# Hybrid decoder step with a mixture of 32 experts: the routing gap reordered, and expert weights fetched in pairs of chunks

## The reference, cut to what matters

```python
g_sel = argmax(hf @ w_rg + b_rg)                        # 1 of 4 groups
e_in  = (hf @ w_re + b_re).reshape(t, 4, 8)[tok, g_sel]
top_v, top_i = lax.top_k(e_in, 2)                       # 2 of its 8 experts
gate  = softmax(top_v) * g_prob[tok, g_sel]
expert = g_sel * 8 + top_i
# for each of 32 experts, on the tokens that chose it:
y = (silu(x @ w1[e]) * (x @ w3[e])) @ w2[e]             # w1, w3: 1024x512, w2: 512x1024
x = x + g2 * sum_k gate_k * y_k
out = rms_norm(x, final_norm_g)
```

## Time and profile before

| | |
|---|---|
| median of 3 runs | 1625.86 us (1625.32 to 1627.21) |
| the profiled execution, its own time | 1624.84 us |
| its span | 1622.9 us |
| PE busy, DVE busy, ACT busy, POOL busy | 96%, 78%, 50%, 18% of the span |
| queue 1 (SP's DMAs) | 196732 packets, 323.89 MB |
| expert weights | 198 DMAs of 1 MB, median 19.1 us from issue to landing |

### The profile page before, as it was taken

One profiled execution on the slowest core, in us unless ns is written; L12 is line 12 of the kernel. 1 busy time (PEld: TensorE's weight loads), 2 busy tenths in 40 slices (PEclk: granted clock), 3 DMA queues, 4 the chain that ended last, 5 costly groups with the idle time before them and its releaser, 6 DMA issues.

```text
span 1622.9 us, 23255 instructions
## 1 busy us (share of the span) xinstructions
PE 1556.6 (96%) x9121; PEld 1338.8 (82%) x9121; DVE 1263.9 (78%) x1695; ACT 808.0 (50%) x871; POOL 296.8 (18%) x240
## 2 busy tenths in 40 slices
PE   6999999999999999999999998999999999999990
PEld 3777788788889999999999977888888888888870
DVE  4668877755838898877455469999999999999975
ACT  4222232335333223323242356878887888777771
POOL 2310000000000000002000202566333233222311
PEclk9999999999999999999999999999999999999995
DMA  9965233424424332225223647999999999999964
GB/s 337 321 199 177 83 85 91 140 80 147 131 85 156 105 91 76 80 88 151 59 85 98 227 183 316 393 379 386 379 378 378 382 376 385 378 376 376 373 231 144
DMA packets 214431, 361.45 MB, mean 223 GB/s; under 512 B 15461, under 2 KB 164021, under 8 KB 188970
## 3 DMA queue, kind: packets, MB, share of 16 engines
q1 hardware_dynamic: 196732, 323.89, 55.6%
q0 software_dynamic: 16944, 33.92, 7.2%
q10 hardware_dynamic: 646, 2.15, 0.3%
HBM read 346.12 MB, written 32.49 MB: 233 GB/s over the span
## 4 chain that ended last, share of the span: by engine, by line
PE 82%; DMA 7%; DVE 7%; issue 1%; ACT 1%; DVEq 1%; SPq 0%; ACTq 0%; POOLq 0%
PE z L2814 16%; PE z L2816 16%; PE z L2815 16%; PE z L896 6%; PE z L894 6%; PE z L895 6%; DMA wr<-in_w_dram 5%; PE z L911 3%; PE z L913 3%; PE z L912 3%; PE q L2705 2%; PE q L2724 1%; PE q L885 1%; DVE wl L1227 1%; DVE conv L2235 1%
## 5 line engine op out<-in xcount | busy, mean ns | idle before, releaser
L1227 DVE TENSOR_TENSOR wl<-wr,whr 128x2048 fp32r<-128x2048 f32 x198 | 446.8, 2284 | 1.3 <-ACT whr L1064 1.3
L1064 ACT ACTIVATE whr<-wr 128x2048 fp32r<-128x2048 f32 x198 | 376.9, 1914 | 81.9 <-DMA wr<-in_w_dram 47.5
L2814 PE MATMUL z<-h_hi,w_hi 128*128 128x272 f32 (+1 forms) x1248 | 406.7, 326 | 2.3 <-DVE h_lo L2054 1.8
L2816 PE MATMUL z<-h_hi,w_lo 128*128 128x272 f32 (+1 forms) x1248 | 402.5, 322 | 0.0
L2815 PE MATMUL z<-h_lo,w_hi 128*128 128x272 f32 (+1 forms) x1248 | 401.3, 322 | 0.0
L2054 DVE TENSOR_TENSOR w_lo<-w_raw,w_hi 128x1024 fp32r<-128x1024 f32 (+1 forms) x168 | 179.4, 1068 | 127.9 <-ACT w_hi L1753 127.9
L2814 PEld LDWEIGHTS z<-h_hi,w_hi 128*128 128x128 f32 x1248 | 234.7, 188 | 28.3 <-issue 7.3
L2816 PEld LDWEIGHTS z<-h_hi,w_lo 128*128 128x128 f32 x1248 | 234.4, 188 | 16.6
L2815 PEld LDWEIGHTS z<-h_lo,w_hi 128*128 128x128 f32 x1248 | 234.8, 188 | 15.7 <-issue 0.2
L894 PE MATMUL z<-whr,xTh 128*128 128x512 f32 x528 | 209.3, 396 | 0.0
L896 PE MATMUL z<-wl,xTh 128*128 128x512 f32 x528 | 206.4, 391 | 0.0
(11 more groups left out here) (457 smaller groups left out, 2222.7 us busy)
## 6 DMA issues: line engine op xcount, KB each, us to landing
wr<-in_w_dram SPq DMA_DIRECT2D x198, 1024.0 KB, 19.1
w_raw<-in_w_in_dram SPq DMA_DIRECT2D x104, 512.0 KB, 3.7
ada<-in_w_ada_dram SPq DMA_DIRECT2D x6, 2048.0 KB, 14.3
w_raw<-in_w_branch_dram SPq DMA_DIRECT2D x48, 256.0 KB, 2.6
w_raw<-in_w_out_dram SPq DMA_DIRECT2D x16, 512.0 KB, 4.0
ada_h<-in_w_ada_dram SPq DMA_DIRECT2D x2, 2048.0 KB, 15.0
ada_u<-in_w_ada_dram SPq DMA_DIRECT2D x2, 2048.0 KB, 9.8
ada_m<-in_w_ada_dram SPq DMA_DIRECT2D x2, 2048.0 KB, 10.6
```

What stands on the lines that cost most here:

```text
L1064: act.activation(whr[n % HN][:], wr[n % RN][:], ACT.Copy).then_inc(m_hi, 1)
L1227: return dve.tensor_tensor(out, a, b, op)
L2814: pe.matmul(out, w_hi[w][:, k, :], hi[:, k, t0:t1], start=(k == 0), stop=False)
L2816: last = pe.matmul(out, w_lo[w][:, k, :], hi[:, k, t0:t1], start=False, stop=(k == kn - 1))
```

## The change

1. `token_ones` makes `ohv` in two parts: `ohv0` for tiles 0 to 3 inside the dense part (after `rank_ones`, L2622), the other five tiles in the gap. PE's L948 matmuls of tiles 0 to 3 wait only for the first.
2. The three memsets on the padding rows of `ohs` go; the matmuls take 32 rows of the last tile instead.
3. The slot table's addresses are made after block 0's work on DVE (`table_rows_of`), POOL's `fill_table` moves from blocks 0 to 8 to blocks 3 to 11, and ACT's first factors wait for `dst_ok`. The overflow list is made after block 4 and read after block 6, its matmul stands on PE in block 5 (in q[1]'s second bank), and `wps` goes from block 2 to 3.
4. `keep_busy` counts: 9 becomes 7, 8 becomes 18 (with the list's matmul gone from behind it), 10 before T(0) becomes 4 after it, 4 becomes 2.
5. Weights are fetched in pairs of chunks: one DMA of 2 MB, 128 partitions of 16 KB, into `wp[i]`, whose halves are `wr[2i]` and `wr[2i+1]`. The ring is 12 chunks (six pairs). A pair's DMA waits until both chunks of the pair that held the slots are finished (m_c of n - 10 for chunks n and n+1), and ACT waits for the whole pair. Six chunks (three pairs) are preloaded; SP issues three pairs when the first gather has landed.
6. The places of `yt`, `fgb`, `x1s`, `g2s` and `ys` are laid out anew; each waits for the same m_c as before or for none.

```diff
-RN = 13
+RN = 12
-        def chunk_dma(eng, dst, e, kind, c, done):
-            if kind == "up":
-                src = expert_rows((w1, w3)[c // 2], e, KD)[:, KF * (c % 2):KF * (c % 2) + KF, :]
-            else:
-                src = expert_rows(w2, e, KF)[:, 2 * c:2 * c + 2, :]
+        def pair_dma(eng, dst, e, kind, c, done):
+            src = expert_rows((w1, w3)[c // 2], e, KD) if kind == "up" else expert_rows(w2, e, KF)
             eng.dma_start(dst[:].rearrange("p (k f) -> p k f", k=src.shape[1]), src).then_inc(done, 16)
...
                 if n >= RN:
-                    sp.wait_ge(m_c, n - RN + 1)
-                chunk_dma(sp, wr[n % RN], e, kind, c, m_ld[n % RN])
+                    sp.wait_ge(m_c, n - RN + 2)
+                pair_dma(sp, wp[n % RN // 2], e, kind, c, m_ld[n % RN // 2])
-            for n in range(5):
+            for n in (0, 2):
                 load(n, CHUNKS[n][0])
             sp.wait_ge(item_mm, 2 * NI)
-            for n in (5, 6, 12):
-                load(n, CHUNKS[n][0])
+            load(4, CHUNKS[4][0])
...
             sp.wait_ge(m_xg[0], 16)
-            for n in (7, 8, 9, 10, 11):
+            for n in (6, 8, 10):
                 load(n, CHUNKS[n][0])
...
-            for n in range(13, 10 * RN):
+            for n in range(RN, 11 * RN, 2):
                 load(n, CHUNKS[n][0])
...
-                act.wait_ge(m_ld[n % RN], 16 * (n // RN + 1))
+                act.wait_ge(m_ld[n % RN // 2], 16 * (n // RN + 1))
...
+        def token_ones(dve, out, t0, t1):
+            shape = [P, t1 - t0, NE]
+            for k in range(2):
+                dve.tensor_scalar(out[:, k, :, 0, :], oh[:, k, t0:t1], vlo[:, 0:1], None, ALU.mult)
+                last = dve.tensor_tensor(out[:, k, :, 1, :], oh[:, k, t0:t1], vhi[:, k, t0:t1].unsqueeze(2).to_broadcast(shape), ALU.mult)
+            return last
...
-            expert_ones(dve, PT, NT)
-            dve.drain()
-            for p0 in range(SMP, P, 32):
-                last = dve.memset(ohs[p0:p0 + 32, NT - 1, :], 0.0)
-            last.then_inc(oh_ok, 1)
+            expert_ones(dve, PT, NT).then_inc(oh_ok, 1)
...
-            keep_busy(pe, 10)
             T(0)
+            keep_busy(pe, 4)
...
+                if b == 0:
+                    table_rows_of()
+                elif b == 3:
...
+                elif b == 4:
+                    overflow_list()
+                elif b == 6:
+                    overflow_rows()
```

More of the change, by code:

```diff
@@ L585, in build @@
         xg0_ok = sem("xg0_ok")
-        m_ld = [sem(f"m_ld{i}") for i in range(RN)]
+        m_ld = [sem(f"m_ld{i}") for i in range(RN // 2)]
         m_xg, m_sc = ([sem(f"{n}{s}") for s in range(2)] for n in ("m_xg", "m_sc"))
@@ L697, in moe_sync @@
                 allow_slow_non_contiguous=True).then_inc(o_i, 16)
-            for n in range(10 * RN, NCH):
+            for n in range(11 * RN, NCH, 2):
                 load(n, CHUNKS[n][0] if CHUNKS[n][0] < NE else e_more)
@@ L719, in moe_sync @@
             scattered(sp, NB - 3)
[L720 to L729, removed]
+            for i in range(4):
+                freed(6 + i)
+                tile_load(2 * i)
+                tile_load(2 * i + 1)
+            freed(10)
             for n_ in range(NS):
@@ L931, in moe_tensor @@
                     pe.matmul(out, oneb[:], ohs[:, j, :], start=False, stop=False)
-                last = pe.matmul(out, tri[:], ohs[:, t, :], start=False, stop=True)
+                rows = P if t < NT - 1 else SMP
+                last = pe.matmul(out, tri[0:rows, :], ohs[0:rows, t, :], start=False, stop=True)
             last.then_inc(q_ready[s], 1)
@@ L937, in moe_tensor @@
             for t in range(PT, NT):
-                last = pe.matmul(q[s][0:NE, 0, 0:1], ohs[:, t, :], oneb[:, 0:1], start=False, stop=(t == NT - 1))
+                rows = P if t < NT - 1 else SMP
+                last = pe.matmul(q[s][0:NE, 0, 0:1], ohs[0:rows, t, :], oneb[0:rows, 0:1], start=False, stop=(t == NT - 1))
             last.then_inc(q_ready[s], 1)
-            keep_busy(pe, 9)
+            keep_busy(pe, 7)
             s = q_wait_free(pe, "tb")
@@ L953, in moe_tensor @@
             pe.matmul(q[s][0:NE, 0, 0:1], trif[:], rowc[:], start=True, stop=True).then_inc(q_ready[s], 1)
[L954 to L957, removed]
+            keep_busy(pe, 18)
             q_wait_read(pe, "tb")
@@ L977, in G @@
                 if b == 0:
-                    q_wait_read(pe, "list")
+                    q_wait_read(pe, "pos")
                 pe.wait_ge(m_g2, b + 1)
@@ L1004, in moe_tensor @@
             last.then_inc(w_ready, 1)
-            keep_busy(pe, 4)
+            keep_busy(pe, 2)
             for b in range(NB):
                 up(b, 0)
+                if b == 5:
+                    q_wait_free(pe, "list")
+                    pe.wait_ge(xls_ok, 1)
+                    pe.matmul(q[1][0:1, 1, 0:MAXX + 1], onef[:, 0:1], xls[:], start=True, stop=True).then_inc(q_ready[1], 1)
                 if b:
@@ L1247, in moe_vector @@
             pick_experts(dve, PT, NT).then_inc(rt_m, 1)
[L1248 to L1252 removed]
+            expert_ones(dve, PT, NT).then_inc(oh_ok, 1)
             dve.wait_ge(he_ok, PT + 1 - NH_D)
[L1254 to L1256 removed]
+            token_ones(dve, ohv, PT, NT)
             dve.drain()
@@ L1325, in moe_vector, with table_rows_of @@
+            def table_rows_of():
+                dve.tensor_scalar(far[:], rk[:], float(P), float(NBLK * P * NE), ALU.is_lt, ALU.mult)
+                dve.drain()
+                dve.scalar_tensor_tensor(far[:], rk[:], float(NE), far[:], ALU.mult, ALU.add)
+                dve.drain()
+                for k in range(2):
+                    last = tt(dsti[:, k, :], far[:, k, :], ef[:, :, k], ALU.add)
+                last.then_inc(dst_ok, 1)
             dve.wait_ge(rt_e, 1)
```

109 lines of the change are left out of this document (55 added, 54 removed).

## The result

The changed kernel takes 1642.01 us (median of 4 runs, 1640.59 to 1643.98) against 1625.99 us for the kernel before in the same session: 1.0097 times the time, 95% interval 1.0084 to 1.0110. It is 16 us slower, outside the predicted range of 1618.5 to 1631, and on the other side of the forecast. The profiled execution has a span of 1638.7 us where the one before has 1622.9.

A forecast was written before the change was run, and what follows sets the result against it. The weight stream was taken to bound the late expert loop, close to PE. Terms -1.3 + 4.9 - 6.3 + 1.9 = -0.8 us gave a median of 1625.1 us, range 1618.5 to 1631.

The forecast's parts named there:

- the queues don't run dry: Weight ring: slots released two chunks later cost nothing, since about eight of 12 are in flight late.
- lumps of two: Late expert loop: both chunks of a pair land together and ACT copies them back to back, +1.9 us, bounds 0 and 4.3.
- what would show the prediction wrong: Signs: 428 GB/s or packets unchanged, flat time in flight, DMA share gaps in the loop, T intervals over 17.75 before 1300.
- Fewer preloads: Before the expert loop's stream: two chunks fewer preloaded, at 2.45 us each, cost +4.9 us.
- Run length: Weight stream: 16 KB runs save 8.2 ns per two 8 KB runs, -6.3 us, bounds 0 and -8.0.
- buys nothing: Rival at the weight stream: 16 KB runs gain nothing over 8 KB, +5.5 us, 1631.4; chance 0.17.
- small fixed part: Rival at the weight stream: a run's fixed part is under half the forecast's, +2.7 us, 1628.6; chance 0.14.
- Landing in pairs: ACT's weight copies late in the loop: both chunks of a pair land together, +1.9 us, bounds 0 and 4.3.
- Start of the stream: Gap before the expert loop: less DVE and PE work brings the first gather 1.3 us earlier, -1.3 us, bounds 0.5 and 2.
- Work moved on DVE and POOL: Gap and early blocks: PE's steady part starts 1 to 2.5 us earlier, but nothing counts at the end.
- The rival on the slower side: Weight stream: run length buys nothing, packets stay 8 KB or cost the same, 1631.4 us; chance 0.17.
- PE-bound rival: Late expert loop: chunks come in under 2.96 us, so PE is the bound again, about 1618.5 us; chance 0.27.

The follow-up runs named there:

- e15: Against e13, a seventh chunk preloaded, chunks 10 and 11 going alone in 8 KB runs: 1628.62 us.
- e8: Weight loads alone, no engine computing, no gathers or scatters, runs of 4, 8 and 16 KB: 998.86 us in all; 410, 422 and 429 GB/s.
- e4: Changed kernel with each pair issued as two 1 MB DMAs of 8 KB runs back to back, each landing on its own semaphore: 1643.95 us.
- e5: Changed kernel's pairs taken apart into single 1 MB chunks on 12 slots, six preloaded, every chunk issued one chunk later: 1631.97 us.
- e14: Against e13, both DMAs of a pair issued at once when the pair's slots are free: 1642.58 us.
- e13: Changed kernel with each pair cut into two DMAs of alternate partitions, 16 KB runs, the second issued one chunk of PE later: 1628.5 us.
- e9: Changed kernel with each pair cut into two DMAs of 64 adjacent partitions, 16 KB runs, the second issued one chunk of PE later: 2053.68 us.
- e7: Kernel before with the reordered gap, single chunks and 13 slots, but six chunks preloaded instead of eight: 1630.62 us.

## Why the prediction was wrong, step by step

The runs form a ladder from the gap-only kernel to the changed one, each step one edit, in medians (the last row is the changed kernel of the first session). Steps between groups come out up to 1.4 us otherwise when they are taken from the ratios, so those of 12 slots and of one DMA can't be told from nothing, and that of the later issue hardly:

| step | us | step alone | predicted |
|---|---|---|---|
| gap reordered, 13 slots, eight preloaded | 1625.6 | -1.0 against the kernel before (0.9994) | -1.3 |
| six preloaded | 1630.6 | +5.0 | +4.9 |
| 12 slots | 1630.8 | +0.2 | 0 |
| issue one chunk later | 1632.0 | +1.2 | 0, "the queues don't run dry" |
| both of a pair must have landed | 1633.7 | +1.8 (alone +2.5) | +1.9 |
| runs of 16 KB | 1628.5 | -5.2 | -6.3 |
| both halves issued at once | 1642.6 | +14.1 | 0, the same sentence |
| one DMA instead of two | 1642.0 | -0.6 | 0 |

- **The step that failed** is the last sentence on lumps of two: "The slots are released two chunks later as well; with 12 slots of which about eight are in flight late (26.0 / 3.08), the queues don't run dry." I had counted what is in flight, found it enough, and put the release at zero. A release that is only later costs 1.2 us, so a chunk of lead is worth little, near the 0 that I gave it. What was missed is that the release in pairs changes the rhythm: 2 MB at once every 6 us instead of 1 MB every 3. That alone is 14.1 us, almost three times the next largest term. And "about eight in flight" holds for the slowest engines only: 26.0 us is the time of the last of 16 steps, and half of the engines have landed a chunk 6.6 us after its issue, with about two in flight. Those engines do run dry. The DMA share of 0.97 in the loop was on my own list of what would show the prediction wrong, though with the shorter ring as its cause; 12 slots for 13 cost 0.2 us, and with 13 the rhythm still costs 11.5. T intervals over 17.75 before 1300 (the chain meets a weight DMA at 1240) and a time in flight that stays flat were on it too, and both came.
- **Fewer preloads**, +4.9: measured +5.0. The argument that the stream rules the end, so a chunk more costs its full transfer, holds here; one preloaded chunk more in e15 was worth nothing, which it does not explain.
- **Run length**, -6.3: 7.8 alone and 5.2 in the loop. The run's fixed part is 2 x 310.6 - 611 = 10 ns (per engine, 16 x 8192 / 422 and 16 x 16384 / 429) instead of 8.2; the 5.2 us in the loop would be 6.8 ns. The rates of 428 and 417 GB/s behind the 8.2 were of windows of 5 and 4 us and 1.4 and 1.7% above what e8 shows over 125 us and more; that the term came out near is in part luck. The rivals "buys nothing" and "small fixed part" are refuted as mechanisms. By the Trainium skill, page "DMA: Bandwidth & Descriptors", section "Why small descriptors are slow", joining pays only up to 256 bytes; the measurement decides against that for runs of 8 KB. Nor does it bear out the 3.5 ns that the prediction worked out from that section.
- **Landing in pairs**, +1.9: measured +1.8 and +2.5.
- **Start of the stream**, -1.3: POOL issues the first gather at 977.60, 0.85 us earlier than in the earlier trace rows and not 1.3, but the gather takes 5.5 us to land where it took 4.5, and its instruction on POOL 2.25 us where it took 1.03; the first pair goes out at 983.17 where the chunk went at 983.00. The term was 0 in place of -1.3; in the kernels with single chunks and the same gap it is -0.2 to -0.7.
- **Work moved on DVE and POOL**, nothing: the gap-only kernel shows it. That PE's steady part would start 1 to 2.5 us earlier was wrong, though: block 14's T stands at 1221.48 in the gap-only kernel and at 1222.44 in the changed one, against 1221.2 before. It had no weight in the sum.
- **The rival on the slower side** gave 1631.4 by the run length; the right rival would have been a stream slowed by its rhythm. The PE-bound rival had no part: PE waits more, not less.

That the rhythm is the cause is shown, twice, with runs of 8 KB (e4 against e5) and of 16 KB (e14 against e13). How it slows the stream is shown in part: around each burst one to two of the 16 engines, four behind three chunks, are idle that are not idle with single issues. It fits that the engines which are ahead finish the last burst before the next is issued, and that capacity lost there does not come back in a stream that needs all of it. Against this as the whole story: over 1300 to 1540 the engines are 1.2% less busy with halves (e4) than with single issues (e5) but move 2.1% less (363.3 against 371.0 GB/s), and a burst of three shows a deeper dip than one of two and costs the same. That stays open, as do how far apart two issues must be (one chunk of PE, 3 us, is enough) and whether the burst would still cost without the gathers and scatters or with a ring several slots longer.

## What to carry to other kernels

When a stream of DMAs runs at full share, look at the rhythm of its issues and not only at how much is in flight: joining two DMAs into one of twice the size also joins their release, and that took 14 us where the longer runs gave 5. The time to landing tells how far the slowest engine is behind, not how much the fastest still has; in this loop it was 24 us against 5, while loads by themselves kept their full rate in DMAs of 2 MB. Before joining transfers, try the rhythm alone, with the DMAs as they are and the waits in pairs; it is an edit of one line. Longer runs can be had without the burst, by cutting the pair by alternate partitions.

## What the runs showed of the hardware that was not expected

- Issuing the second of two 1 MB DMAs 3 us **later** made the kernel 12 us (8 KB runs) and 14 us (16 KB runs) faster, with chunks 20 to 22 us in flight (8 KB runs, e5 and e4).
- The 16 steps in which a 1 MB DMA lands are spread over 19 us in the loop of the kernel before (5.4 to 24.4 us after its issue) and over about 1 us for a 2 MB DMA in the loads alone (28.2 to 29.4).
- DMAs that write 64 adjacent partitions each moved 215 to 226 GB/s in the loop at a DMA share near 1, where the same bytes over alternate partitions moved 372 to 384 (e9 and e13, 1000 to 1500). The rate falls to six tenths although the DMAs of the two halves are on their way together: one is issued every 5.3 us and takes 14.5 us or more to land. By the Trainium skill, page "SBUF — State Buffer", section "Door 1: The DMA port swizzle", bit 6 of the partition number picks one of the two ports of a pair, so 64 adjacent partitions reach 8 of 16 ports and every second one reaches all; both runs agree with it.
- A run of 16 KB still gains 1.7% over 8 KB (429 against 422 GB/s), and 8 KB 2.9% over 4 KB (410), the DMA growing with the run.
- One slot of lead less costs 0.2 to 1.2 us in this stream-bound loop, and each of two chunks not preloaded 2.5 us (e7), while one preloaded more in e15 gave nothing.
